# Transposes as four 64x64 products with an identity, each half of the rows with a PSUM bank of its own

## The reference

```
z = x @ w_in                      # q, k, v, g, a_low, conv b/c/h, xq
y_gla  = gated linear attention (4 heads, dk 64, dv 128), rms norm, silu gate
y_conv = c_b * causal_conv3(c_c * c_h)
y_xa   = softmax(xq . mk^T / 8) . mv      # 4 heads, 256 memory tokens, mk|mv = mem @ w_mem_kv
x1 = LN1(alpha * x + [y_gla | y_conv | y_xa] @ w_out)
x2 = LN2(alpha * x1 + relu(x1 @ w_ff1)^2 @ w_ff2)
```

## Time and profile before

| | |
|---|---|
| median of 3 runs | 2207.67 us (2207.6 to 2208.45) |
| profiled execution, its own time | 2207.49 us |
| its span, first to last instruction | 2205.8 us |
| PE busy | 2125.3 us, 96% of the span |
| DVE, ACT, POOL busy | 1383.5, 1010.9, 522.4 us |
| mean granted clock of TensorE | 0.988 |

### The profile page before, as it was taken

How to read it: one execution, slowest core, us unless ns; L and a number is a source line. 1 busy time by engine, 2 the same in 40 slices (tenths; PEclk the granted TensorE clock), 3 DMA queues, 4 the chain that set the end, 5 groups by cost and what they waited for, 6 DMA issues and landing times.

```text
span 2205.8 us, 28174 instructions
## 1 busy us (share of the span) xinstructions
PE 2125.3 (96%) x11008; PEld 1705.7 (77%) x11008; DVE 1383.5 (63%) x1902; ACT 1010.9 (46%) x1360; POOL 522.4 (24%) x483
## 2 busy tenths in 40 slices
PE   7999999999999999899999999999999999999996
PEld 5777787778777777678888788888788888778885
DVE  3667566756765677655556667565575644964458
ACT  4534454444444445445445554444443333633334
POOL 3002001101010213020100244444494800710004
PEclk9999999999999999899999999999999999999998
DMA  6123323323331523254645777868868665665553
GB/s 193 58 61 95 95 86 122 109 77 116 96 115 58 170 60 125 73 209 160 214 151 183 266 272 256 279 238 282 330 212 286 195 193 195 216 226 191 194 196 135
DMA packets 241060, 374.21 MB, mean 170 GB/s; under 512 B 16368, under 2 KB 117776, under 8 KB 240928
## 3 DMA queue, kind: packets, MB, share of 16 engines
q1 hardware_dynamic: 212096, 272.68, 37.7%
q0 software_dynamic: 28832, 99.74, 12.8%
HBM read 272.74 MB, written 99.61 MB: 169 GB/s over the span
## 4 chain that ended last, share of the span: by engine, by line
PE 49%; DVE 6%; issue 3%; DMA 2%; ACT 2%; POOL 0%; DVEq 0%; SPq 0%; ACTq 0%; POOLq 0%
PE main L68 8%; PE main L69 8%; PE main L70 8%; PE sc L68 6%; PE sc L69 6%; PE sc L70 6%; DVE w_lo L1565 3%; PE aux L69 1%; PE ob L69 1%; PE aux L70 1%; PE ob L70 1%; PE ob L68 1%; PE aux L68 1%; DMA w_b<-in_w_ff_dram 1%; DMA x_ops<-xop_dram 1%
## 5 line engine op out<-in xcount | busy, mean ns | idle before, releaser
L1565 DVE TENSOR_TENSOR w_lo<-w_b,w_hi 128x1024 fp32r<-128x1024 f32 x144 | 216.8, 1508 | 248.2 <-ACT w_hi L1535 248.2
L1565 DVE TENSOR_TENSOR w_lo<-raw,w_hi 128x1024 fp32r<-128x1024 f32 x144 | 206.4, 1438 | 126.0 <-ACT w_hi L1535 126.0
L1535 ACT ACTIVATE w_hi<-raw 128x1024 fp32r<-128x1024 f32 x144 | 152.4, 1059 | 251.4 <-PE main L70 117.5
L1535 ACT ACTIVATE w_hi<-w_b 128x1024 fp32r<-128x1024 f32 x144 | 152.3, 1058 | 176.8 <-PE aux L70 78.5
L1051 DVE TENSOR_TENSOR w_lo<-raw,w_hi 128x1024 fp32r<-128x1024 f32 x116 | 141.5, 1227 | 145.3 <-ACT w_hi L754 144.0
L68 PE MATMUL main<-xT_lo,w_hi 128*128 128x512 f32 (+1 forms) x528 | 219.5, 416 | 1.5 <-DVE xT_lo L1063 1.5
L70 PE MATMUL main<-xT_hi,w_hi 128*128 128x512 f32 (+1 forms) x528 | 207.8, 394 | 0.0
L69 PE MATMUL main<-xT_hi,w_lo 128*128 128x512 f32 (+1 forms) x528 | 207.6, 393 | 0.0
L68 PE MATMUL main<-x_lo,w_hi 128*128 128x512 f32 x448 | 179.1, 400 | 9.5 <-ACT z L1886 7.5
L68 PE MATMUL sc<-x_lo,w_hi 128*128 128x512 f32 x448 | 178.2, 398 | 8.5 <-DVE x_lo L1508 5.7
L68 PE MATMUL main<-w_lo,w_hi 128*128 128x512 f32 x448 | 175.8, 392 | 5.0 <-DVE w_lo L1565 4.9
(11 more groups left out here) (255 smaller groups left out, 4712.1 us busy)
## 6 DMA issues: line engine op xcount, KB each, us to landing
raw<-in_w_in_dram SPq DMA_DIRECT2D x80, 512.0 KB, 3.7
h_dram<-z SPq DMA_DIRECT2D x64, 512.0 KB, 3.8
raw<-h_dram SPq DMA_DIRECT2D x112, 256.0 KB, 2.7
w_b<-h_dram SPq DMA_DIRECT2D x112, 256.0 KB, 2.7
h_dram<-h_s SPq DMA_DIRECT2D x48, 512.0 KB, 5.0
rows<-in_x_dram POOLq DMA_DIRECT2D x32, 512.0 KB, 5.0
raw<-in_w_out_dram SPq DMA_DIRECT2D x32, 512.0 KB, 3.7
raw<-in_w_ff_dram SPq DMA_DIRECT2D x32, 512.0 KB, 6.4
```

What stands on the lines that cost most here:

```text
L1535: act.activation(ff.w_hi[:, n % RING, :], slot_tile(ff, m), ACT.Copy).then_inc(ff.hi_done, 1)
L1565: dve.tensor_tensor(ff.w_lo[:, n % RING, :], slot_tile(ff, m), ff.w_hi[:, n % RING, :].bitcast(F32), ALU.subtract).then_inc(ff.lo_done, 1)
```

## The change

Each burst of eight transposes becomes 32 products of 64x64 with the matching quarter of `ident`. Rows 0 to 63 of the source go to bank 0 and rows 64 to 127 to bank 1, where before each bank held four whole transposes. Both banks are finished at the end of a burst, and PE waits for both to be free ahead of it. The copies out of the banks write runs of 64 elements in place of 128. The feed-forward pieces are loaded so that features 0 to 511 lie on partitions 0 to 63 and features 512 to 1023 on partitions 64 to 127: still four DMAs of the same size a piece, each now to 64 partitions.

```diff
@@ transposes
                 for b in range(2):
                     pe.wait_ge(sc_free[b], u_sc)
-                    for k in range(4):
-                        src = rows[:, j, P * (4 * b + k):P * (4 * b + k) + P]
-                        ins = pe.transpose(sc[b][:, P * k:P * k + P], src, ident[:, :])
-                    ins.then_inc(sc_done[b], 1)
+                for k in range(KT):
+                    for part in range(2):
+                        cols = slice(P * k + 64 * part, P * k + 64 * part + 64)
+                        for b in range(2):
+                            half = slice(64 * b, 64 * b + 64)
+                            ins = pe.matmul(sc[b][64 * part:64 * part + 64, 64 * k:64 * k + 64], rows[half, j, cols],
+                                            ident[half, half], start=True, stop=True)
+                            if k == KT - 1 and part == 1:
+                                ins.then_inc(sc_done[b], 1)
@@ xattn_transpose
                 pe.wait_ge(xp_ready, 4 * t + j + 1)
+                for b in range(2):
+                    pe.wait_ge(sc_free[b], SC_USES * t + 2 + SC_XA + 2 * j + 1)
                 for m in range(2):
-                    pe.wait_ge(sc_free[m], SC_USES * t + 2 + SC_XA + 2 * j + 1)
                     for h in range(4):
-                        ins = pe.transpose(sc[m][:, P * h:P * h + P], xp[:, h, P * m:P * m + P], ident[:, :])
-                    ins.then_inc(sc_done[m], 1)
+                        for part in range(2):
+                            cols = slice(P * m + 64 * part, P * m + 64 * part + 64)
+                            at = slice(64 * (4 * m + h), 64 * (4 * m + h) + 64)
+                            for b in range(2):
+                                half = slice(64 * b, 64 * b + 64)
+                                ins = pe.matmul(sc[b][64 * part:64 * part + 64, at], xp[half, h, cols],
+                                                ident[half, half], start=True, stop=True)
+                                if (m, h, part) == (1, 3, 1):
+                                    ins.then_inc(sc_done[b], 1)
@@ xT_part on ACT (DVE's has the same slices)
-                act.activation(xT_hi[:, 4 * b:4 * b + 4, P * j:P * j + P],
-                               sc[b][:, :].rearrange("p (k n) -> p k n", k=4), ACT.Copy).then_inc(xt_hi_done, 1)
+                act.activation(xT_hi[:, :, P * j + 64 * b:P * j + 64 * b + 64],
+                               sc[b][:, :].rearrange("p (k n) -> p k n", k=KT), ACT.Copy).then_inc(xt_hi_done, 1)
@@ the copy of the transposed probabilities on ACT (DVE's is of the same form)
-                    act.activation(xpT[:, 0, :], sc[0][:, :], ACT.Copy).then_inc(sc_free[0], 1)
+                    act.activation(xpT_half[0], sc[0][:, :].rearrange("p (m h n) -> p m h n", m=2, h=4), ACT.Copy
+                                   ).then_inc(sc_free[0], 1)
@@ load_x_piece
-            src = normed[t0:t0 + 256, 512 * j + P * kt:512 * j + P * kt + P].rearrange("(a p) n -> p a n", p=P)
-            eng.dma_start(dst[:, k, :, j, :], src).then_inc(ff.x_piece_landed[at], 16)
+            src = normed[t0:t0 + 256, 512 * j + P * kt:512 * j + P * kt + P].rearrange("(a p) n -> p a n", p=64)
+            eng.dma_start(dst[64 * j:64 * j + 64, k, :, :], src).then_inc(ff.x_piece_landed[at], 16)
@@ x_transposes
-    for j in range(2):
-        for t in range(4):
-            ins = pe.transpose(banks[j][:, P * t:P * t + P], src[:, t, j, :], ff.ident[:, :])
-        ins.then_inc(ff.xg_done, 1)
+    for t in range(8):
+        for part in range(2):
+            for j in range(2):
+                half = slice(64 * j, 64 * j + 64)
+                ins = pe.matmul(banks[j][64 * part:64 * part + 64, 64 * t:64 * t + 64],
+                                src[half, t, 64 * part:64 * part + 64], ff.ident[half, half], start=True, stop=True)
+                if t == 7 and part == 1:
+                    ins.then_inc(ff.xg_done, 1)
```

More of the change, by code:

```diff
@@ L207, in hybrid_layer @@
         probs = xpT[:, 0, 0:2 * CH]
+        xpT_half = [xpT[:, :, :].rearrange("p m (h b n) -> p m h b n", h=4, b=2)[:, :, :, b, :] for b in range(2)]
         mkT = sb("mkT", [P, 2, M])
@@ L1061, in xT_part @@
                 dve.wait_ge(xt_hi_done, n + 1)
-                dst = (slice(None), slice(4 * b, 4 * b + 4), slice(P * j, P * j + P))
-                dve.tensor_tensor(xT_lo[dst], sc[b][:, :].rearrange("p (k n) -> p k n", k=4), xT_hi[dst].bitcast(F32),
+                dst = (slice(None), slice(None), slice(P * j + 64 * b, P * j + 64 * b + 64))
+                dve.tensor_tensor(xT_lo[dst], sc[b][:, :].rearrange("p (k n) -> p k n", k=KT), xT_hi[dst].bitcast(F32),
                                   ALU.subtract).then_inc(sc_free[b], 1)
@@ L1268, in mixer_block @@
                     dve.wait_ge(sc_done[1], SC_USES * t + 2 + SC_XA + 2 * j + 2)
-                    dve.tensor_copy(xpT[:, 1, :], sc[1][:, :]).then_inc(sc_free[1], 1)
+                    dve.tensor_copy(xpT_half[1], sc[1][:, :].rearrange("p (m h n) -> p m h n", m=2, h=4)
+                                    ).then_inc(sc_free[1], 1)
                     if j == 0:
@@ L1431, in load_x_piece @@
 def load_x_piece(eng, ff, normed, q, half, at):
-    dst = ff.x_piece_of[at][:, :].rearrange("p (k a j n) -> p k a j n", k=2, a=2, j=2)
+    dst = ff.x_piece_of[at][:, :].rearrange("p (k a n) -> p k a n", k=2, a=4)
     quarter, kt = q % 2, q // 2 % 4
@@ L1446, in x_transposes @@
     use = PIECE_USE[q] if q < X_STEPS else q - 3
-    src = ff.x_piece_of[at][:, :].rearrange("p (t j n) -> p t j n", t=4, j=2)
+    src = ff.x_piece_of[at][:, :].rearrange("p (t n) -> p t n", t=8)
     pe.wait_ge(ff.x_piece_landed[at], 64 * (use + 1))
```

## The result

The changed kernel takes 2227.65 us (median of 4 runs, 2225.89 to 2229.12) against 2208.06 us for the kernel before on the same chip: 19.6 us slower, ratio 1.0085, 95% interval 1.0071 to 1.0099. The forecast was 2225.6, 17.9 us slower.

What follows compares the result with a forecast made beforehand. PE, busy 96% of the span, was taken as the bound. 15.4 us for bursts outside block 0 plus 2.5 in it gave 17.9 on 2207.49, thus 2225.4, and 2225.6 as median; range 2214 to 2235 (8 in 10).

Steps and rivals of the forecast that it cites:

- The burst: PE's step over a burst: 1.73 us against 1.35, 0.38 more, reckoned from the existing float32 64x64 `score` products, edges included.
- The bounds from 0.07 to 0.62: Extra us per burst on PE: 0.07 if edges cost nothing, 0.62 if L547 hides in the score.
- How many count: Of 50 bursts, 39 pay 0.38 each, 14.8 us; input waits add 0.2 and `mem` 0.4, together 15.4.
- The feed-forward's 16: Between mixer and feed-forward, five bursts hide in waits for `rows` and `x_lo`; 11 x 0.38 count.
- Block 0 apart: Four input bursts where the loop PE, ACT, DVE, PE is the path: 12.4 us instead of 9.9, 2.5 more.
- the clock only as a rival with a gain: Block 0: products keep TensorE's clock up, giving back up to 2.9 us, 2222.7; chance 0.08. Opposite case adds up to 3.4.
- `mem`: Two bursts on the path at the start of the kernel: 0.4 us more for both.
- Terms at nothing: Copies out of the banks, their split among engines and the feed-forward piece loads: taken as 0 us.
- The loads: Feed-forward piece loads, landing in 5.1 us before: taken as 0, with some 4 us kept for the range.
- One pass with free edges: Rival at all bursts: products go through once, 2205 us; with free edges too, 2197. Chance of one pass 0.09.
- A round of 0.218 us: Rival at all bursts: four products take 0.218 us by the transpose-mode rule, total 2256; chance 0.01.
- Covering waits in the attention: Rival: waits for `xpT` (5.6) and `v_rows` (5.1) swallow up to 10.7 us of added work, 2215; chance 0.13.

Runs made afterwards that it cites:

- the doubled burst: Kernel before with only the softmax probabilities changed, each burst issuing its 32 products twice: 2228.97 against 2210.84 us, ratio 1.0083.
- runs six and seven: Kernel before, probabilities in 64-row by 128-column halves: as transposes 2208.66 us (ratio 0.9996), as float32 products with the identity 2230.65 (1.0090), against 2210.84.
- run three: Kernel before with the change in the feed-forward pieces and their loads alone: 2214.37 us, ratio 1.0027.

## Why the prediction was right

- **The burst**, 0.38 dearer from the score's rows: 0.40 measured, in all three places. The missing 0.02 is the product behind the burst, 0.34 to the next, where I had put the score's 0.32. That it is the edges and not the rounds was shown by the doubled burst. The bounds from 0.07 to 0.62 weren't needed.
- **How many count**: the 24 bursts of blocks 1 to 3 pay in full, 9.6 us. The wait at the second input burst of a block grew from 0.90 to 1.08, with the first burst's 0.40 swallowed, as written, so that a block's four input bursts cost 1.6. The four bursts of probabilities in block 0 don't pay in full, which I had overlooked: PE waits 0.6 to 1.25 us for `xp` ahead of each, before and after (the earlier trace rows has their sum, 3.2), and the edge ahead of the burst hides there. They cost 0.9 together and not 1.6.
- **The feed-forward's 16**: the count was 11, 4.4 us; alone they measured 5.6 (4.0 to 8.2). In the profile of the change the first of these bursts starts 19.3 us later than in the kernel before (874.1 and 854.8), the last 18.6 later, so in this pair of profiles the 16 cost nothing: the waits were shorter (3.2 in all, where I had 1.9), and a stretch at half clock was missing. That is this pair's luck. From the first of them to the last it is 336.3 to 340.1 us over seven profiles with whole transposes and no fillers there (the kernel before has the 340.1) and 339.5 to 341.3 over five with products, on average 1.6 more.
- **Block 0 apart** is the term that was off: 2.5 us forecast, 4.9 measured for the loop and 4.3 with the large products behind it. Without the half clock a turn of the loop is 3.3 us and not 3.1, since ACT starts 1.28 and not 1.18 after the burst: 3.3 more for the four. The rest is TensorE's clock, 1.6 in the loop and 1.0 in all. I had the clock only as a rival with a gain and, on the other side, as a mishap of up to 3.4.
- **`mem`** was 0.4. From its first burst to the first product of the weights it is 7.0 us before and 8.1 after (7.66 to 15.80), which looks like 1.2. But the same stretch was 6.5 to 10.1 us over ten profiles in which these bursts are whole transposes, so neither number is shown.
- **Terms at nothing.** The sum came closer than its terms. The two profiles' spans are 20.7 us apart: 1.8 up to block 0's first input burst, 4.3 in block 0 up to the large products, 1.1 in the rest of block 0, 9.6 in the bursts of blocks 1 to 3, 2.4 in longer waits for `v_rows`, -0.3 in the feed-forward's bursts, and 1.8 behind the last of them, where nothing was changed. The forecast had 2.5 for block 0, 4.2 for the feed-forward and nothing for the 2.4 and the 1.8. What carries the forecast is the burst's price and the count outside block 0 and the feed-forward; that the whole came within 2 us is in part luck, as these other errors cancel.
- **The loads** of the pieces to 64 partitions landed in 5.8 us (5.1 before): 5.7 to 5.9 in the six profiles that have them, 4.8 to 5.4 in the other eight. PE waited for them 1.0 us or less in all.
- **Rivals.** One pass with free edges fell: two instructions a product, edges at 0.32 and 0.34. A round of 0.218 us, by the Trainium skill's rule that transpose mode is four times faster for float32 ("TensorE: Matmul & The Clock Gate", Terms), fell too, as the round of quarters took 0.117; where the shape was the same with and without that mode, in runs six and seven, the step from round to round was 3.6 times shorter with it (0.063 and 0.224), which is near that rule. Covering waits in the attention (`xpT` 5.6 to 5.7, `v_rows` 5.1 to 7.5) gave nothing back.
- **The clock** went the other way. The half-clock stretch of block 0 was 13.7, 13.7 and 17.1 us in the three profiles with products there and no fillers. In the seven with whole transposes and no fillers it was 6.8 or 10.2, and in one of them (run three) it was missing; it was missing in all four profiles with fillers. So products don't keep the clock up where transposes don't, as one would expect if transposes alone didn't count as PE work (the Trainium skill, "TensorE: Matmul & The Clock Gate", Part 4). With work in the gaps the clock stayed up; that the change lengthens the stretch by lengthening PE's idle time is the likely reading, from three profiles.

Open: the wait for `v_rows` was 2.3 to 9.1 us over the fourteen profiles. In block 3 it ends with ACT, which is held up by the landing of a weight load (13.6 us before, 15.3 in the change). The four kernels with the change in all three places, or in all but block 0 and `mem`, have the longest, 7.5 to 9.1; the other ten have 2.3 to 7.4. Whether the change lengthens it isn't shown. It is large enough to hide or feign an effect of this change's size.

## What to carry to other kernels

Packing four small float32 products into the array wasn't cheaper here than a whole transpose: a round of four costs what one transpose costs (0.117 and 0.109 us), and the other tile shape is paid for at both ends of every burst, which with the rounds makes 0.4 us, so short bursts between large products are a bad place for it. When a kernel has the same kind of instruction somewhere already, cut its price from two products around it, edges included, not from its duration. If two banks are finished together where they used to be finished one after the other, the evacuation starts later by half a burst, which costs only where nothing else stands between the bursts. A forecast is checked term by term: one pair of profiles can hide a term of 4 us or feign one of 1, so a stretch is to be looked up in every profile that has the same code there.

## What was not expected of the hardware

- In block 0 of the kernel before PE stood idle for 1 to 1.5 us behind each burst, and the clock then fell to 1.2 GHz (so in six of seven profiles with this code). With 0.9 us of useless products in each gap 2.4 GHz stayed in block 0, and the kernel before was 5 to 6 us faster (0.25%, 0.15 to 0.36), twice what the half-clock stretch there explains (2.7, the difference of block 0 with and without fillers); the rest isn't explained.
- Tiles of 64 rows by 128 columns pay the same edges as quarters (0.33 ahead, 0.15 and 0.34 behind), as transposes and nearly so as products (0.20 in place of 0.15).
- Float32 products of that shape took three times as long as transposes of it (1.94 and 0.64 us for the same 16 pieces; from round to round 0.224 and 0.063), though they appear as only twice the instructions.
